# A two-pass feed-forward stage on one core: high parts of weight blocks move to another engine, and down products move in the order

## The reference, cut to what matters

```
h = _rmsnorm(x, norm_ffn_g)
u = jnp.einsum('bsd,df->bsf', h, w_up)
up = jnp.pad(u, ((0, 0), (1, 1), (0, 0)))
u = up[:, :-2] * conv_w[0] + up[:, 1:-1] * conv_w[1] + up[:, 2:] * conv_w[2] + conv_b
a, b = jnp.split(u, 2, axis=-1)
x = x + jnp.einsum('bsf,fd->bsd', jax.nn.silu(a) * b, w_down)
...
return _rmsnorm(x, final_norm_g)
```

## Time and profile before

| | us |
|---|---|
| median of 3 runs | 2541.35 |
| the profiled execution's own time | 2539.73 |
| its span | 2537.8 |
| PE busy | 2400.6 (95%) |
| DVE busy | 1733.7 (68%) |
| POOL busy | 1554.1 (61%) |
| ACT busy | 895.5 (35%) |

### The profile page before, as it was taken

One profiled execution on the slowest core, in us unless ns is written; L12 is line 12 of the kernel. 1 busy time (PEld: TensorE's weight loads), 2 busy tenths in 40 slices (PEclk: granted clock), 3 DMA queues, 4 the chain that ended last, 5 costly groups with the idle time before them and its releaser, 6 DMA issues.

```text
span 2537.8 us, 33971 instructions
## 1 busy us (share of the span) xinstructions
PE 2400.6 (95%) x12402; PEld 2047.8 (81%) x12402; DVE 1733.7 (68%) x2407; ACT 895.5 (35%) x1706; POOL 1554.1 (61%) x1779
## 2 busy tenths in 40 slices
PE   7999999999999899999999999999799999999997
PEld 6999999998988788888888777787677777777775
DVE  7536676788889843343333788765777778777777
ACT  4335555556678831233322122111211111111113
POOL 4453644788778320331501666666888888888886
PEclk9999999999999999999999999999999999999998
DMA  8643434432212162222443322221411111111112
GB/s 302 226 171 135 150 124 165 160 126 92 80 40 81 32 218 75 99 76 80 149 139 129 111 82 98 86 91 67 166 42 46 50 42 49 47 50 50 45 43 88
DMA packets 102581, 260.40 MB, mean 103 GB/s; under 512 B 10128, under 2 KB 45328, under 8 KB 91920
## 3 DMA queue, kind: packets, MB, share of 16 engines
q1 hardware_dynamic: 101120, 257.82, 29.5%
q10 hardware_dynamic: 1296, 0.39, 0.1%
HBM read 209.95 MB, written 48.23 MB: 102 GB/s over the span
## 4 chain that ended last, share of the span: by engine, by line
PE 47%; DVE 9%; ACT 4%; issue 3%; POOL 2%; DMA 0%; DVEq 0%; ACTq 0%; POOLq 0%; SPq 0%
PE r_bank L2023 19%; PE r_bank L1929 10%; PE r_bank L1900 9%; PE r_bank L1962 5%; DVE r_conv L2318 4%; DVE r_conv L2380 2%; ACT r_conv L2204 2%; DVE r_g_lo L2383 1%; PE r_bank L1981 1%; PE r_bank L2010 1%; PE r_bank L1944 1%; ACT r_conv L2218 1%; ACT r_g_hi L2220 1%; DVE r_rows L2448 1%; DVE r_rows L2405 1%
## 5 line engine op out<-in xcount | busy, mean ns | idle before, releaser
L832 PE MATMUL t_proj<-t_w_hi,t_hbuf 128*128 128x384 f32 x1056 | 311.0, 348 | 0.7 <-DVE t_hbuf L1075 0.5
L2388 DVE TENSOR_TENSOR r_x_p<-r_bank,r_x_p 128x512 f32<-128x512 f32 x320 | 211.3, 685 | 70.9 <-PE r_bank L2023 67.7
L1129 DVE TENSOR_REDUCE t_max_neg<-t_scores 128x1 f32<-128x1024 f32 (+1 forms) x192 | 197.7, 1038 | 33.3 <-PE t_scores L863 32.6
L996 ACT ACTIVATE t_prob<-t_scores,t_max_neg 128x1024 f32<-128x1024 f32 (+1 forms) x192 | 187.4, 977 | 67.2 <-DVE t_max_neg L1129 63.5
L832 PEld LDWEIGHTS t_proj<-t_w_hi,t_hbuf 128*128 128x128 f32 x1056 | 196.3, 190 | 3.5 <-issue 0.7
L1149 DVE TENSOR_TENSOR t_pt_lo<-t_turn,t_pt_hi 128x512 fp32r<-128x512 f32 x240 | 163.2, 686 | 47.1 <-ACT t_pt_hi L1005 44.7
L2318 DVE SCALAR_TENSOR_TENSOR r_conv<-r_rows,r_taps,r_conv 128x511 f32<-128x511 f32 (+1 forms) x132 | 167.6, 1269 | 40.5 <-ACT r_conv L2204 38.2
L1723 POOL TENSOR_TENSOR r_stat<-r_stat,minus_half 128x1 f32<-128x1 f32 x24 | 14.1, 587 | 273.1 <-DVE r_stat L2281 273.0
L832 PE MATMUL t_proj<-t_w_lo,t_hbuf 128*128 128x384 f32 x528 | 178.9, 339 | 0.0
L1005 ACT CAST t_pt_hi<-t_turn 128x512 fp32r<-128x512 f32 x240 | 139.6, 588 | 97.6 <-PE t_turn L876 85.3
L1778 POOL TENSOR_TENSOR r_w_lo<-r_stage,r_w_hi 128x1024 fp32r<-128x1024 f32 (+1 forms) x86 | 166.1, 1931 | 7.2
(11 more groups left out here) (295 smaller groups left out, 7365.7 us busy)
## 6 DMA issues: line engine op xcount, KB each, us to landing
t_hbuf<-split_x SPq DMA_DIRECT2D x60, 1024.0 KB, 4.8
r_stage<-in_w_up_units SPq DMA_DIRECT2D x44, 512.0 KB, 3.3
r_rows_w<-in_w_up_units SPq DMA_DIRECT2D x88, 256.0 KB, 2.9
split_x<-t_hbuf SPq DMA_DIRECT2D x12, 1024.0 KB, 4.9
r_stage<-in_w_down SPq DMA_DIRECT2D x22, 512.0 KB, 3.3
r_wd_raw<-in_w_down SPq DMA_DIRECT2D x42, 256.0 KB, 2.9
t_stage<-in_w_in_units SPq DMA_DIRECT2D x6, 1536.0 KB, 6.5
t_xkv_raw<-in_w_xkv_heads SPq DMA_DIRECT2D x16, 512.0 KB, 6.4
```

Source lines behind the costliest of these rows:

```text
L832: ins = nc.tensor.matmul(proj_bank(i), l, r[:, k, :], start=(k == 0 and j == 0), stop=(k == KT - 1 and j == 2))
L996: nc.scalar.activation(prob[:, n % PSLOTS, 0:p.keys], ps_s[:, n % 2, 0:p.keys], ACT.Exp, bias=max_neg[:, n % COLS:n % COLS + 1], accum_out ...
L1129: nc.vector.tensor_reduce(max_neg[:, n % COLS:n % COLS + 1], ps_s[:, n % 2, 0:p.keys], AX.X, ALU.max, negate=True).then_inc(max_done, 1)
L2388: nc.vector.tensor_tensor(x_p[:, t, cols], down_bank(n), x_p[:, t, cols], ALU.add).then_inc(p_add, 1)
```

## The change

In the second pass all nine high parts of a step (w11, w12, w22, s1 to s4, and two halves of the down weights) become copies on ACT (`rows_hi`, `sum_hi`, `down_hi`); POOL keeps sums and low parts. s2 no longer reads s1's sum: POOL adds w21 and w22 a second time in s2's own buffer and subtracts w11 (`s2_sum`), so that s2 is ready first and s1 later. One function, `operand_orders`, holds the order of sums, high parts and low parts from which the semaphores' values come. The operands' buffers move: w11 to 156, s2 to 160, s1 and w22 to 164, w12 and s4 to 168, s3 to 188. The first operands of step 0 are made within the last step of the first pass. PE's 16 down products of a step stand beside w12, s3, w22 and s4. DVE's adds move with them, and c12 comes before the low part of the edge columns. In the first pass the eight down products start behind k = 3 of the second up product, two at a time at first.

```diff
+W_OPERANDS = {"w11": 156, "s2": 160, "s1": 164, "w22": 164, "w12": 168, "s4": 168, "s3": 188}
+SAMPLE_WEAVE = {3: (0, 1), 4: (2, 3), 5: (4, 5), 6: (6,), 7: (7,)}
...
@@ SP: load_rows, load_down
                 elif name == "w12":
-                    sp.wait_ge(s4_begun, i)
+                    sp.wait_ge(op_sum, sum_at["s4a", i - 1])
+                    sp.wait_ge(op_ready, ready_at["w12", i - 1])
+                elif name == "w11":
+                    sp.wait_ge(op_sum, sum_at["s3", i - 1])
+                    sp.wait_ge(op_ready, ready_at["w11", i - 1])
...
@@ POOL
-            def halves(hi, lo, raw):
-                stepped(nc.gpsimd.tensor_scalar(hi[:, :], raw[:, :], 1.0, 1.0, ALU.mult, ALU.mult))
-                return nc.gpsimd.tensor_tensor(lo[:, :], raw[:, :], f32(hi[:, :]), ALU.subtract)
+            def low(i, name, raw):
+                pool.wait_ge(op_hi, hi_at[name, i])
+                nc.gpsimd.tensor_tensor(wop_lo[name][:, :], raw[:, :], f32(wop_hi[name][:, :]), ALU.subtract).then_inc(op_ready, 1)
...
+            def s2_sum(i):
+                for name in ("w11", "w21", "w22"):
+                    pool.wait_ge(rows_in[name], 16 * (i + 1))
+                slot_free(i, "s2", "s2")
...
+                nc.gpsimd.tensor_tensor(raw[:, :], w_rows["w21"][:, :], w_rows["w22"][:, :], ALU.add).then_inc(op_sum, 1)
+                pool.wait_ge(op_sum, sum_at["s2a", i])
+                nc.gpsimd.tensor_tensor(raw[:, :], raw[:, :], w_rows["w11"][:, :], ALU.subtract).then_inc(op_sum, 1)
...
+            def down_low(i, c):
+                pool.wait_ge(wd_rounded, 2 * i + c + 1)
...
                 split_down(i, 0)
                 if i < LAST:
                     split(i + 1, 1)
+                else:
+                    rows_low(0, "w11")
+                    s2_sum(0)
+                    sum_low(0, "s2")
+                    s1_sum(0)
+                    sum_low(0, "s1")
                 split_down(i, 1)
...
@@ PE
                 for k in range(KT):
                     sample_up(i, 1, k)
-                    sample_down(i - 1, k)
+                    for n in SAMPLE_WEAVE.get(k, ()):
+                        sample_down(i - 1, n)
...
-                        elif 0 < i < LAST and 2 <= o < 6:
-                            prompt_down(i - 1, HK * (o - 2) + k)
+                        elif 0 < i < LAST and o >= 3:
+                            prompt_down(i - 1, HK * (o - 3) + k)
...
@@ ACT
+            def sum_hi(i, name):
+                act.wait_ge(op_sum, sum_at[name, i])
+                nc.scalar.copy(wop_hi[name][:, :], wop_raw[name][:, :]).then_inc(op_hi, 1)
+
+            def down_hi(i, c):
+                act.wait_ge(wd_in[c], 16 * (i + 1))
...
                     nc.scalar.activation(conv[:, 0, edge], conv[:, 0, edge], ACT.Silu).then_inc(edge_silu, 1)
+                    if i:
+                        down_hi(i, 0)
+                    if i == LAST:
+                        down_hi(i, 1)
+                    else:
+                        sum_hi(i + 1, "s2")
+                        sum_hi(i + 1, "s3")
                     act.wait_ge(c22_done, i + 1)
                     act.wait_ge(c21_done, i + 1)
                     mid(i, 1, whole, value[:, :], value_mid)
+                    if i < LAST:
+                        sum_hi(i + 1, "s1")
...
@@ DVE
                     nc.vector.tensor_tensor(gate[:, second], one_bank(PRODUCT_BANK["s4"]), gate[:, second], ALU.add).then_inc(c12_done, 1)
+                    gated_low(i - 1, edge, edge_hi, edge_split)
                     dve.wait_ge(late_mid, i)
...
```

More of the change, by code:

```diff
@@ L1486, in rest_phase @@
         last_mean, last_rstd, scaled, out_a, out_b, y_sent = (sem(n) for n in ("last_mean", "last_rstd", "scaled", "out_a", "out_b", "y_sent"))
-        def ready_at(i, name):
-            late = ("w22", "s4")
-            if name in late:
-                return NP * i + 6 + late.index(name)
-            return NP * i + 1 + (("w11", "s3", "s2", "s1", "w12") if i else ("w11", "s2", "s1", "w12", "s3")).index(name)
+        sum_order, hi_order, lo_order = operand_orders()
+        sum_at, hi_at, ready_at = ({step: n + 1 for n, step in enumerate(o)} for o in (sum_order, hi_order, lo_order))
         def done_at(i, name):
@@ L2418, in _ @@
                 if i:
[L2419 removed]
+                    gated(i - 1, rest, late_silu, late_prod)
+                    gated_low(i - 1, rest, late_hi, late_split)
                 else:
```

204 lines of the change are left out of this document (120 added, 84 removed).

## The result

| | before | after |
|---|---|---|
| median, us | 2541.32 (4 runs) | 2439.45 (4 runs, 2438.85 to 2440.01) |
| span of the profiled execution, us | 2537.8 | 2438.0 |

What follows compares the result with a forecast made beforehand. It took PE as the bound, with gaps set by POOL's list and a DVE/ACT chain; -4 - 8 - 67.4 - 1 = -80.4 from 2539.73 gave 2459.3, or 2461 with the median's 1.6, stated as 2460, range 2446 to 2494.

Steps and rivals of the forecast that it cites:

- First pass: Down product 0 moves 2.0 us later, so its 0.19 us wait goes in 21 steps: -4 us, bounds 0 and -4.5.
- Between the passes: From the first pass's last matmul to s1 of step 1, today's gaps of 21.8 us become 13.6: -8 us.
- Loop A: Second pass: from down product 7's end through down weights, ACT, POOL and DVE to c12, 16.3 us, just closing.
- Loop B: Second pass: POOL's own list from the late high part to the next down low part, ending 0.3 us too late.
- the second mis-sized term: Second pass, s1 of step 1 to s1 of step 21: period 30.3 us, 20 times, -67.4 us.
- Rival 2: Second pass: no loop binds, period 29.9 us and the best start, 2447 to 2450 us; chance 0.12.
- The collisions: Second pass: POOL and DVE instructions delay each other; about half of ten DVE instructions a step meet POOL, period 30.3.
- "idle POOL" argument: Second pass: DVE's edge product, edge low part and late shifts fall where POOL waits for ACT; edge product about 0.57 us.
- rival 1: Second pass: POOL and DVE meet as often as now, period 31.8 us, 2490 us in all; chance 0.26.
- Step 21 and the end: Last step and end: c12 earlier, s4's operand a little late, `value_mid` behind two copies: -1 us, bounds +2 and -2.
- the signs that I named: Period 30.3, down product 3's wait under 0.5, PE waiting for c12, `value_mid` behind s3, POOL about 20 us, first-pass steps 16.3.

Runs made afterwards that it cites:

- e1_weave: The kernel before, with only PE's eight sample downs moved behind k = 3 of the second up product, two at a time at first: 2521.61 us.
- e3_first_pass: The kernel before, with PE's sample downs and DVE's sample adds both reordered as in the change's first pass, nothing else: 2521.52 us.
- e10_dose3: The changed kernel with three more copies of s3's high part on ACT ahead of `value_mid`, in steps 2 to 21: 2476.15 us.
- The doses: The changed kernel with one or three extra ACT copies a step (2449.41, 2476.15 us), or 256 or 512 extra POOL columns (2450.63, 2461.42 us).
- e7_pool_high: The changed kernel with all nine high parts of a step back on POOL, each directly ahead of its low part: 2452.08 us.

## Why the prediction was wrong, step by step

**What bounds it.** Right: PE with gaps set by loops over POOL, ACT and DVE, and PE's pace of 29.9 as the floor.

**First pass: the step that failed.** "In the first pass PE has no idle time but one place of 0.87 in place of 0.68 us", times 21. I read one late step and took it for all. The stretch in the earlier trace rows was the same late step, and the low part's place behind "one add of 0.64 us" left the four extra instructions out, though the diff shows them in the loop that it moves. The piece of 1.37 us stands in the chain 11 times. The 11 steps that hold it take 17.97 us each, the nine late ones 16.52, and PE's own work is 16.32: 18.2 and 1.8 us, the 20.0 of the table. e1_weave and e3_first_pass measured 19.5. This term put the time out of the range: with the 16 us back it would have been 2455. Its bounds were 0 and -4.5.

**Between the passes.** -8 said, -7.1 found. The walk's gaps stand in the trace at their places: 0.61 at s2 (0.7 said), 1.35 at s1 (2.1), 3.55 at s4 (4.6) and 6.42 at s1 of step 1 (3.7). The last was longer than said, the others shorter. The low clock behind s4 cost 1.7 us (2.5 said; 12 matmuls from 1768.43 to 1772.88 in place of 2.7). That the wait at s1 would cost clock too I had not seen: the 12 matmuls from 1784.93 take 4.8 us, 2.1 more than at full clock, and they lie in the next stretch of the table.

**Loop A** was walked at 16.3 us against 16.3, no room. The trace has 15.7, and 0.15 more until PE could start: in e10_dose3 c12 ends at 2070.34 and s1 starts at 2070.48. I had added durations and 0.3 us of hand-overs on top, for which no row stood. The rows follow each other more closely than their durations say: `value_mid` starts 0.53 us behind the start of s3's copy of 0.62, and c12 0.46 behind that of the edge product of 0.54. The doses say up to 0.26 of room. **Loop B** was walked 0.3 too long; the doses say the same room. Its own stretch I had right: from the late high part to s4's low part it is 12.1 us (0.62 + 10.3 + 1.2). The trace has 12.1, from the start of ACT's copy to the end of the low part that is POOL's last ahead of the down weights':

```profile
2061.24 0.62 ACT L2227 CAST r_wd_hi<-r_wd_raw 128x512 fp32r<-128x512 f32 x1
```

```profile
2072.06 1.30 POOL L1810 TENSOR_TENSOR r_s_lo<-r_s_raw,r_s_hi 128x512 fp32r<-128x512 f32 x1
```

What I had wrong by half a microsecond was how the two loops lie against PE's own work. That is the second mis-sized term: 30.3 said, 29.9 measured, 20 times, 7.6 us, less the 2.1 of low clock at its start, so 5.5 us. Rival 2, no loop binds, had the second pass right, and I gave it 0.12: with both loops within 0.3 us of PE's own period on my paper, a difference of that size was not to be had from a walk, and 29.9 deserved as much as 30.3.

**The collisions** went as the "idle POOL" argument said: 0.54 for the edge product (0.57 said), 0.56 for the edge low part, 0.83 for the late one. e7_pool_high has them back, with 1.10, 1.69 and 1.74 us, and its period is 30.55, not the 31.8 of rival 1. It is no clean test of that rival, since it also takes the copies' hand-overs off both loops.

**What the prediction did not price** is each part of the second pass by itself. Undone alone, the copies on ACT cost 0.62 us a step, c12's place 0.8, the later down products and adds 1.35, s2's own sum 5.9, of which 3.5 are idle time. They don't add up to the 3.8 gained, since each leaves another bound behind. The new places of the buffers, and SP's new waits that go with them, were not tried alone.

**Step 21 and the end**: -1 said, -1.5 found. The 1.8 us by which the code ahead of the first pass took longer are between two executions; nothing there was changed. Of the signs that I named, the wait at down product 3 is gone, `value_mid` stands behind s3's copy, POOL is busy 21.1 us a step and a first-pass step takes 16.3; PE's wait at s1 for c12, the one that was to remain, is gone too.

## What to carry to other kernels

Before a stall read in one step is multiplied by the number of steps, look for the same piece in the first, a middle and the last step of the loop: a step that does extra work for a later stage is bound by something else. When a loop over other engines comes out within a few tenths of the bound engine's own period, give both cases like chances, and measure the room with two doses of extra work, since one dose alone does not tell room from slope. And move both sides of a pair (products and the adds that free their banks) or neither.
